# A retention and mixture-of-experts layer on one core: the last norm placed inside the "no further round" branch, the clearing of a scratch tensor moved, and the first norm's waits loosened

## The reference, cut to what matters

```
h  = layer_norm(x)                          # first norm, gain and offset ln_in
z  = h @ w_in                               # q, k, v, gate, GLU pair, two merge gates
A  = retention(q, k, v) -> norm -> * silu(gate) -> @ w_ret_out
B  = GLU -> causal depthwise conv, 31 taps -> norm -> silu -> @ w_conv_out
h1 = layer_norm(alpha*h + (sig(ga)*A + sig(gb)*B) @ w_out)
m  = experts(h1)                            # 4 groups x 8 experts, each token goes to 2 of the 32
pe = (p @ w_ple_proj) * sigmoid(h1 @ w_ple_gate)
y  = layer_norm(alpha*h1 + m + pe)          # last norm, gain and offset ln2
```

## Time and profile before

| | us |
|---|---|
| median of 3 runs | 899.08 (898.63 to 900.42) |
| the profiled execution's own time | 896.93 |
| its span, first to last instruction | 895.1 |
| PE busy | 850.2 (95%) |
| DVE busy | 389.9 (44%) |
| ACT busy | 291.8 (33%) |

### The profile page before, as it was taken

One profiled execution on the slowest core, in us unless ns is written; L12 is line 12 of the kernel. 1 busy time (PEld: TensorE's weight loads), 2 busy tenths in 40 slices (PEclk: granted clock), 3 DMA queues, 4 the chain that ended last, 5 costly groups with the idle time before them and its releaser, 6 DMA issues.

```text
span 895.1 us, 14908 instructions
## 1 busy us (share of the span) xinstructions
PE 850.2 (95%) x6064; PEld 521.5 (58%) x6064; DVE 389.9 (44%) x740; ACT 291.8 (33%) x330; POOL 74.5 (8%) x93
## 2 busy tenths in 40 slices
PE   8999999999999999999999999999999998989975
PEld 3899777888998997754443444434443443434331
DVE  5779998998683566761111112110210030110126
ACT  4433225556646733343222123121321231111110
POOL 1200000001111000051000000000000000000000
PEclk7999999999999999999999999999999999999988
DMA  9853535777899768929999999999999999999991
GB/s 314 296 190 142 146 137 178 194 189 213 221 280 291 183 235 346 420 105 367 377 420 421 421 421 420 419 423 422 421 420 423 423 420 421 422 420 422 420 335 63
DMA packets 43444, 286.44 MB, mean 320 GB/s; under 512 B 6391, under 2 KB 6647, under 8 KB 10241
## 3 DMA queue, kind: packets, MB, share of 16 engines
q1 hardware_dynamic: 36034, 254.58, 71.3%
q0 software_dynamic: 7072, 29.07, 13.4%
q10 hardware_dynamic: 288, 2.10, 0.6%
HBM read 258.78 MB, written 14.45 MB: 305 GB/s over the span
## 4 chain that ended last, share of the span: by engine, by line
PE 59%; DMA 22%; DVE 3%; issue 1%; SPq 0%; ACT 0%; ACTq 0%; POOLq 0%; DVEq 0%
DMA raw_x<-wstream 20%; PE ps L1645 17%; PE ps L1665 6%; PE ps L1356 6%; PE ps L1358 5%; PE ps L1357 5%; PE ps L1614 4%; PE ps L1580 4%; PE ps L1388 2%; PE ps L1389 1%; PE ps L1390 1%; PE ps L1383 1%; DMA y_second<-y_tok 1%; PE ps L1651 1%; PE ps L1398 1%
## 5 line engine op out<-in xcount | busy, mean ns | idle before, releaser
L1645 PE MATMUL ps<-raw_x,xs 128*64 128x512 f32 x1008 | 235.1, 609 | 19.5 <-DMA raw_x<-wstream 19.5
L1645 PEld LDWEIGHTS ps<-raw_x,xs 128*64 128x64 f32 x1008 | 71.2, 139 | 137.2 <-issue 134.9
L954 DVE SCALAR_TENSOR_TENSOR cT_sb<-uT_sb,conv_par,cT_sb 128x350 f32<-128x350 f32 x240 | 120.7, 575 | 1.1 <-issue 0.5
L1665 PE MATMUL ps<-raw_x,actT 128*64 128x512 f32 x504 | 113.7, 593 | 0.0
L598 ACT ACTIVATE w_hi<-raw_dense 128x2048 fp32r<-128x2048 f32 x40 | 76.4, 1910 | 68.4 <-PE ps L1383 40.9
L1356 PE MATMUL ps<-hT_hi,w_hi 128*128 128x320 f32 x304 | 95.9, 316 | 2.2 <-issue 2.2
L1357 PE MATMUL ps<-hT_lo,w_hi 128*128 128x320 f32 x304 | 94.0, 309 | 0.0
L1123 DVE TENSOR_TENSOR onehot<-iota_r,rankm 128x192 bf16<-128x192 f32 x33 | 11.8, 359 | 163.6 <-PE ps L1614 163.5
L1358 PE MATMUL ps<-hT_hi,w_lo 128*128 128x320 f32 x256 | 79.2, 309 | 0.0
L1665 PEld LDWEIGHTS ps<-raw_x,actT 128*64 128x64 f32 x504 | 36.3, 137 | 71.5 <-issue 68.8
L1261 DVE TENSOR_TENSOR act_rows<-ps,gate_silu 64x512 f32<-64x512 f32 x32 | 22.2, 694 | 126.4 <-ACT gate_silu L771 126.4
(11 more groups left out here) (280 smaller groups left out, 1079.7 us busy)
## 6 DMA issues: line engine op xcount, KB each, us to landing
raw_x<-wstream SPq DMA_DIRECT2D x189, 1024.0 KB, 22.8
raw_dense<-wstream SPq DMA_DIRECT2D x43, 1024.0 KB, 6.9
w_lo<-raw_dense POOLq DMA_DIRECT2D x11, 1024.0 KB, 9.3
w_lo_third<-raw_dense POOLq DMA_DIRECT2D x6, 1024.0 KB, 10.2
raw_extra<-wstream SPq DMA_DIRECT2D x3, 1024.0 KB, 7.6
y_tok<-nothing POOLq DMA_DIRECT2D x2, 1280.0 KB, 9.0
raw_dense<-wstream ACTq DMA_DIRECT2D x2, 1024.0 KB, 12.2
const<-consts SPq DMA_DIRECT2D x1, 1297.5 KB, 15.7
```

What stands on the lines that cost most here:

```text
L954: i = stt(out=cT[:, j, :], in0=src, scalar=w, in1=cT[:, j, :], op0=ALU.mult, op1=ALU.add)
L1645: i = mm(ps[64 * h:64 * h + 64, 1 + odd, :], x, w[h][:, k, :], start=half == 0 and k == 0, stop=half == 1 and k == 3)
L1665: i = mm(ps[64 * h:64 * h + 64, 4 + par, :], a, w[:, f, h, :], start=j == 0 and f == 0, stop=j == 1 and f == 1)
```

## The change

- `WARM[0]` goes from 5 to 2: two calls of the fillers on zeros at the start in place of five.
- ACT's `root(0)` stands ahead of the four copies of gain and offset, not behind them.
- DVE's first norm waits for two of these copies (the gain) ahead of its first instruction and for all four ahead of its second; before, for all four ahead of the first.
- PE's `proj(0)` waits for the first of the copies; the wait for all four stands behind it, ahead of the first transposes.
- The clearing of `nothing` goes from behind chunk 0's low part into the loop at i = 3, ahead of the conv taps, and the taps there go from eight to three. The five taps left out fall to i = 28.
- On DVE and PE the end (`finish()`, `sums()`) is placed inside the branch for no further round, which now comes first; the further rounds, followed by a second copy of the end, are in its `Else`. PE runs six calls of the fillers ahead of `sums()` in the first branch. ACT, SP and POOL keep their branches.

```diff
-WARM = (5, 3, 3, 1, 5, 0, 0, 0, 15, 5)
+WARM = (2, 3, 3, 1, 5, 0, 0, 0, 15, 5)
@@ scalar
+        root(0)
         for n in range(4):
             act.wait_ge(ss("ln_psum"), n + 1)
             go(ln_in_gb[:, n // 2, ...], ps[:, n, :], ACT.Copy).then_inc(ss("ln_copied"), 1)
-        root(0)
         proj_copy(0)
@@ vector, norm_tile
             link(stt(out=tmp[0:q, :], in0=src, scalar=mv[0:q, t, 0:1], in1=gb[0:q, 0, :],
                      op0=ALU.subtract, op1=ALU.mult))
+            if beta:
+                dve.wait_ge(ss("ln_copied"), beta)
             stt(out=rows[0:q, t, :], in0=tmp[0:q, :], scalar=rstd[0:q, t:t + 1], in1=gb[0:q, 1, :],
                 op0=ALU.mult, op1=ALU.add).then_inc(ss(out_sem), 1)
@@ vector
             if t == 0:
-                dve.wait_ge(ss("ln_copied"), 4)
-            norm_tile(t, ln_in_gb, "h_rows", ln_tmp, rows[0:ROWS[t], t, :])
+                dve.wait_ge(ss("ln_copied"), 2)
+            norm_tile(t, ln_in_gb, "h_rows", ln_tmp, rows[0:ROWS[t], t, :], beta=4 if t == 0 else 0)
         lo(0)
-        V.memset(nothing[:], 0.0).then_inc(ss("nothing_set"), 1)
-        TAPS_AT = {i: 8 for i in range(3, 9)}
+        TAPS_AT = {3: 3, **{i: 8 for i in range(4, 9)}}
@@ vector, loop over chunks
+            if i == 3:
+                V.memset(nothing[:], 0.0).then_inc(ss("nothing_set"), 1)
             conv(TAPS_AT.get(i, 0))
@@ vector, end
-        with dve.If(flag > 0):
+        with dve.If(flag < 1):
+            finish()
+        with dve.Else():
+            link.n, roots[0] = steps, begun
             with dve.Fori(1, ROUNDS) as r:
                 rounds(r)
-        (the three acc, then the three last norms)
+            finish()
@@ tensor, start
-        pe.wait_ge(ss("ln_copied"), 4)
+        pe.wait_ge(ss("ln_copied"), 1)
         pe.wait_ge(ss("ple_in"), 16)
         pe.wait_ge(raw_d_in[3], 16)
         proj(0)
+        pe.wait_ge(ss("ln_copied"), 4)
         pe.wait_ge(ss("ident_in"), 16)
@@ tensor, end
-        with pe.If(flag > 0):
+        with pe.If(flag < 1):
+            keep_warm(6, bank=6)
+            sums()
+        with pe.Else():
             with pe.Fori(1, ROUNDS) as r:
                 rounds(r)
-        (the sums of the three tiles)
+            sums()
```

More of the change, by code:

```diff
@@ L869, in layer_norm, with norm_tile @@
             after(2)
-        def norm_tile(t, gb, out_sem, tmp, src):
+        def norm_tile(t, gb, out_sem, tmp, src, beta=0):
             q = ROWS[t]
@@ L1328, in rounds, with finish @@
             aT_copy(r * EXPERTS + EXPERTS - 1)
+        def finish():
+            dve.wait_ge(ss("base_ready"), TILES)
+            for t in range(TILES):
+                acc(t)
+            dve.wait_ge(ss("ln2_in"), 16)
+            for t in range(TILES):
+                dve.wait_ge(ss("sum_psum"), t + 1)
+                number = rows_begin(t, src=sum_psum(t))
+                dve.wait_ge(ss("root_out"), number)
+                link(V.reciprocal(rstd[:, t:t + 1], rstd[:, t:t + 1]))
+                norm_tile(t, ln_gb, "final_rows", ln2_tmp, sum_psum(t))
         rounds(0)
@@ L1332, in _ @@
         flag = dve.value_load(more[0:1, 0:1], min_val=0, max_val=1)
-        with dve.If(flag > 0):
+        steps, begun = link.n, roots[0]
+        with dve.If(flag < 1):
+            finish()
+        with dve.Else():
+            link.n, roots[0] = steps, begun
             with dve.Fori(1, ROUNDS) as r:
                 rounds(r)
[L1338 to L1347, removed]
+            finish()
     @block.tensor
@@ L1712, in rounds, with sums @@
             down(r, EXPERTS // 2 - 1, 0, 0, n0 + EXPERTS - 1)
+        def sums():
+            pe.wait_ge(ss("last_ready"), 1)
+            for t in range(TILES):
+                q = ROWS[t]
+                pe.wait_ge(ss("acc_ready"), t + 1)
+                for c in range(2):
+                    mm(sum_psum(t)[:, 512 * c:512 * c + 512], ident[0:q, 0:q], base_rows[0:q, t, 512 * c:512 * c + 512], start=True, stop=False)
+                for c in range(2):
+                    pe.wait_ge(ss("y_kept"), 2 * LAST - 1 + c)
+                    m = mm(sum_psum(t)[:, 512 * c:512 * c + 512], last_wT[:, 128 * t:128 * t + q], y_last[:, 512 * c:512 * c + 512],
+                           start=False, stop=True)
+                m.then_inc(ss("sum_psum"), 1)
         rounds(0)
```

## The result

The changed kernel took 891.93 us (median of 4 runs, 890.68 to 895.73) against 899.75 (4 runs, 898.63 to 900.75) for the kernel before: a ratio of 0.9926 [0.9900 to 0.9952] (in square brackets the 95% interval), 7.8 us less. Run again beside the first experiments it took 892.94 (10 runs) against 899.69 (33 runs): 0.9922 [0.9898 to 0.9946], 7.0 less. The forecast was 894.1, a gain of 5.0; the first measurement lies just under the lower end that the prediction gave, 892.2, and the second inside.

What follows compares the result with a forecast made beforehand. PE's dense-stage progress sets when the DMA-bound expert weight stream gets going; a serial end follows. Front 3.1 plus end 1.9 gives 5.0: profiled 896.93 becomes 891.9, plus 2.15 to the median, 894.1; range 892.2 to 897.4.

Steps and rivals of the forecast that it cites:

- Rivals 1 and 4: Start: clock rises no sooner than before (895.3, chance 0.13); TensorE stays at 1.2 GHz through the projections (903.4, chance 0.06).
- rival 4: From proj(0) to chunk 0: TensorE stays at 1.2 GHz through the projections, 4.3 us slower, 903.4; chance 0.06.
- the feared collision: Chunk 4: POOL's later addition could run beside DVE's low part, losing 0.8 us; zero was taken.
- Should arrive whole at 846 us: Weight stream's end: time won ahead of chunk 1 (3.1 us) arrives there undiminished, although the stage between is DMA-bound.
- the prediction's own sign: Forecast is wrong if first expert wait for DMA and stream's end do not move by the same amount as chunk 1.
- the front: Start plus clearing, up to chunk 1: 1.9 + 1.18 = 3.1 us gained, bounds 1.9 and 4.0.
- rival 3: Between chunk 1 and the end: the 3.1 us gained early is absorbed in DVE-limited chunks or the ring; 897.2, chance 0.08.
- The reading of the flag: Behind the last expert on PE: 1.05 us for reading and branching, 4.6 for the far jump that leaves the path.
- rival 2: End gives nothing back: PE stays at 1.2 GHz, or DVE's jump over the Else becomes far; 896.0, chance 0.14.
- cannot move: End: DVE's additions wait for rows read from DRAM (6.6 us), end at 875.20, limiting the end's gain to 1.9 us.

Runs made afterwards that it cites:

- DVE's order: Changed kernel with VectorE's work at the end reordered (first tile's statistics between the additions, gain wait at first use): 890.38 us, 0.9899 against the kernel before.

## Why the prediction came out as it did

**The start.** Every forecast for the start's timeline held: one table load fewer on ACT, fillers to 2.9 (3.1), slow spreading and `proj(0)` at 10.1 (10.17), second tile at 12.4 (12.18), the clock's rise at 15.1 (15.3), chunk 0 at 25.4 (25.34), chunk 1 at 32.7 without idle time (32.46). The new start gave chunk 0 at 24.84 to 25.87 in the five traces that have it with two fillers; the old one 27.34, 27.59, 27.63 and 25.73 in the kernel before, and 28.76 twice where the spreading was slow. Rivals 1 and 4, a rise no sooner or none at all, did not occur: in these five traces the clock rose between 14.3 and 16.4. The nearest to rival 4 is the old order with two fillers, where it came at 20.3. The reason that the prediction gave, no more holes in PE's work, is not shown as the cause: in the quickest repeat of the kernel before, PE stood idle for 1.06 and 0.32 us and the clock rose at 15.3 as well, where the earlier trace rows has 18.5. That the forecast hit 15.1 so closely is in part luck. That repeat, by stretch (columns as above):

```profile
14.00:15.00 1.00, 0.68 (x4) 0.54 (x4) 0.96 (x3) 0.60 (x1) 0.26 (x1) 0.50 0.98 410
15.00:16.00 1.00, 1.00 (x8) 0.97 (x7) 0.93 (x3) 0.00 (x0) 1.00 (x2) 0.85 1.02 426
```

That the same program shows different moments of the rise is what the Trainium skill says ("TensorE: Matmul & The Clock Gate", Part 1: The HAM clock gate), and the four traces of the kernel before agree: the rise came at 15.3 in one and at 18.5 to 19.2 in three, chunk 0 at 25.73 against 27.34 to 27.63.

Taken over these traces, chunk 24 is done at 241.37 with the new start (five traces) and at 244.94 with the old start and clearing (before, its three repeats and the end alone): 3.6 us, where 3.1 was forecast. Without the one old start among them that spread slowly it is 3.2; slow spreading behind five calls is what the one profile of before could not show.

**The clearing.** The idle 1.18 ahead of chunk 1 went, as forecast. From the end of chunk 0 to that of chunk 1 it gave a little more, 1.41: 7.04 us in every trace that has the edit, 8.45 to 8.48 in every one that has not. POOL's addition at 54.02 fell just behind chunk 4's low part (51.60, 2.29 long), so the feared collision did not happen, and DVE still waits 4.08 for PE at i = 28 (6.56 before): the five taps lie in its idle time, as forecast. The row of the changed kernel:

```profile
277.39 3.52 DVE L1177 TENSOR_TENSOR cT_sb<-cT_sb,ps 128x350 f32<-128x350 f32 x8 [4.08 <-PE ps L1542]
```

**"Should arrive whole at 846 us"** is the step that the pair contradicts and the timed runs bear out. By the prediction's own sign (the stream's end moves as far as chunk 1) it would be wrong in this pair. The lead was 3.40 at chunk 1 and 3.42 at chunk 24 (241 us). In chunks 25 to 27 PE then stood idle for 2.5 against 1.5 us, and the lead was 2.34. The routing stage took 34.85 against 33.23 us, by the half-clock stretches shown above (7.0 us at a mean of 0.51 against 3.7 us at 0.54), and 0.7 was left; at the last expert's end it was 0.3 (865.64 and 865.93), where the forecast had 3.1. By these two traces the front is absorbed, which is rival 3. But the start and clearing alone took 5.0 off the timed runs (3.1 to 7.0 by the interval), so it is not. The length of the routing stage is not fixed by the code: it took 32.0 us in six of the thirteen traces, 33.2 in two and 34.85 in five, and among the five traces with the same code up to there (the new start with two fillers) 34.85 three times and 32.0 twice. With the new order of the start it was long in four traces of six, with the old in one of seven; that is too few to say whether the new start makes it more likely. In one repeat of the kernel before the granted clock never fell there:

```profile
380.00:387.00 7.00, 7.00 (x44) 4.69 (x43) 6.41 (x17) 4.34 (x5) 5.66 (x8) 1.00 0.98 405
```

That single executions are 2.9 apart by such a draw is shown; why the clock falls in one and not in another was not tried.

**The end.** The mechanism was right, the size was not. PE stood idle for 5.66 to 6.73 us around the jump in the traces with the old end, and not at all with the new one. The timeline has only "issue" for this time, but the DMA table shows a packet on a queue of instructions in it. From the last expert's end to PE's return in the trace of before (866 to 871.59; queue, packets, MB, share of the 16 engines):

```profile
q8 instruction: 1, 0.02, 1.5%
```

In all seven traces with the old end one such packet of 16 KB starts 2.5 to 3.6 us behind the last expert's end, and PE is back 3.0 to 3.2 us after that start; in the six with the new end none starts within 10 us. So the jump's price goes with a load of instructions, though the table does not say for which engine. Whether a shorter body behind the branch would make it cheaper was not tried.

The reading of the flag, for which 1.05 was set aside, shows nothing on PE (fillers at 865.57, last expert to 865.64). The statistics do stand directly behind DVE's last addition, and DVE's jump over the `Else` shows nowhere: rival 2 is out, as the end alone gained 2.9. But 1.9 came from one execution whose end was short. From the last expert to the last landing of y it is 28.8 us there, and 29.6 on average in the seven traces with the old end (28.5 to 30.8), and 27.1 in the five with the new one in the change's DVE order (26.6 to 27.7): 2.5, not 1.9. The missing part goes with the half clock after the jump, which reached well into the second half of the first tile's sums in two of the repeats and in the run with two fillers (2.8 to 3.1 for it, against 1.9 to 2.2 in the other four). In the pair itself only 1.1 came, as the rows read from DRAM made DVE wait 7.8 and not 6.6: the forecast that the additions "cannot move" held for their order, not for the moment at which the rows land. The Trainium skill's rule ("Runtime: NRT & Kernel Launch", Instruction fetch mechanics), that a taken branch out of the fetched stretch stalls the engine, agrees with PE's 5.66 here; for DVE's branch no run here shows such a stall.

**The sum.** Corrected terms: 3.6 + 2.5 = 6.1, forecast 5.0, measured 7.8 and 7.0, with intervals that reach from 4.3 to 9.2. The remaining 1 to 2 us are not placed by these means, and in the same traces the lead shrinks from 3.6 at chunk 24 to 1.5 at the last expert's end. One reason is which executions were traced: the three of the new start with a routing stage of 34.85 took 2.1 to 3.8 us longer than the medians of their kernels, the two with 32.0 lie within 0.4 of theirs. Two traces that stand near the medians of their kernels, the first repeat of before (900.03) and the changed kernel without end fillers (892.82), both with 32.0 in the routing stage, account for the whole gain. Their last matmuls of the last expert:

```profile
863.67 3.65 PE L1665 MATMUL ps<-raw_x,actT 128*64 128x512 f32 x16
...
860.16 3.65 PE L1674 MATMUL ps<-raw_x,actT 128*64 128x512 f32 x16
```

The lead is 3.1 at chunk 24, 3.1 at the first expert and 3.5 here, and the end gives 3.9 more (30.5 and 26.6 us to the last landing): 7.4, by their times 7.2. There the front arrives whole, and the term that the forecast had too small is the end, 1.9 where it measures 3.9. It is one pair, on two chips; over many executions the split stays open.

## What to carry to other kernels

A taken branch over a long body can cost the engine that takes it several us even if the body never runs (here PE, 5.7 to 6.7): put the usual case directly behind the test, and look whether another engine's wait becomes the limit, since that is where the next gain lies (here DVE's order, a further 2.1 to 2.4). Before a gain of a few us is worked out from one trace, compare several of the unchanged kernel: a stage that varies by 3 us with the clock hides it in a single pair, and a term read off one short execution is too small. Filler matmuls are to be judged with the order behind them; here taking them out gave at most 3.0 us by itself and nothing that its trace shows.

## What was not expected of the hardware

- TensorE's clock can fall while PE is busy. In the trace of before the granted clock fell at 8.3, while the last of the eight matmuls on one stationary row was still running and PE had had no hole since 1.3; the prediction read this as a fall behind them. In the routing stage it stood at 0.51 over 7.0 us in which PE was busy for 7.00. The eight matmuls took either 3.8 to 4.2 or 7.19 us: behind two filler calls 7.19 in six traces of six, behind five in three of seven, and these three are not of the chip on which the three repeats were quick.
- The granted clock's column is not to be trusted ahead of the first change on record: it reads 1.00 from 3.05 to 10.20 in the trace after, where the eight matmuls run at half clock: one takes 1.06 us, against 0.59 at a granted 1.00 in the trace of before. In the trace after, the record begins with the rise at 15.3.
- The half-clock stretches in the routing stage, together 0, some 3.7 or some 7 us long in the traces looked at, are one draw of the whole time's scatter: 2.9 us between the extremes. A further one, some 3.3 us long, stands between 243 and 267 us in six of the thirteen traces.
